# Encoder block on one core: projections as a stage from high and low parts, the delta rule on 64x64 blocks pipelined across units, gate projections in attention

## What is computed

```python
mod = silu(c) @ w_ada + b_ada          # shift1, scale1, gate1, shift2, scale2, gate2
h = rmsnorm(x) * (1 + scale1) + shift1
proj = h @ w_in                        # qkv_a, z_a, beta, alpha, q_b, k_b, v_b, gate_a, gate_b
# A: 4 heads of 128: conv of 5 taps on q, k, v, silu, l2norm of q and k, then per direction,
#    in chunks of 64 tokens (strict, incl: lower triangles; g: cumulated log-decay)
lower = where(strict, beta * (k @ k.T) * exp(g_i - g_j), 0)
u, w = solve(lower + I, [beta * v, beta * exp(g) * k])
for each chunk:                        # S: 128 x 128 state
    v_new = u - w @ S
    o = (q * exp(g)) @ S + (q @ k.T * decay) @ v_new
    S = S * exp(g_last) + (k * exp(g_last - g)).T @ v_new
o_a = rmsnorm(o_forward + o_backward) * gn_w * silu(z)
# B: neighbourhood attention, 8 heads of 64, on the 8 x 64 token grid, window 8 x 16, with a bias
merged = sigmoid(gate_a) * (o_a @ w_oa) + sigmoid(gate_b) * (o_b @ w_ob)
x = x + gate1 * (merged @ w_out)
# then a mixture of 16 SwiGLU experts, each on its top 64 tokens of the group, and a final norm
```

## Time and profile before

| | us |
|---|---|
| median of 3 runs | 2817.16 |
| lowest, highest | 2816.36, 2833.86 |
| the profiled execution | 2837.16 |
| its span, first to last instruction | 2835.4 |

### The profile page before, as it was taken

How to read it: one execution, slowest core, us unless ns; L and a number is a source line. 1 busy time by engine, 2 the same in 40 slices (tenths; PEclk the granted TensorE clock), 3 DMA queues, 4 the chain that set the end, 5 groups by cost and what they waited for, 6 DMA issues and landing times. The chain is left out here.

```text
span 2835.4 us, 32777 instructions
## 1 busy us (share of the span) xinstructions
PE 2648.7 (93%) x11148; PEld 1771.3 (62%) x11148; DVE 1575.7 (56%) x1868; ACT 1177.4 (42%) x1392; POOL 451.4 (16%) x373
## 2 busy tenths in 40 slices
PE   7999999999999997899889859999999999999994
PEld 2465546646564654566334448888888888888883
DVE  2343334434343442344121168888888888888884
ACT  2222121212212221444111137777767776666773
POOL 2022020202110220100122310111111111111101
PEclk9999999999999999555899969999999999999997
DMA  6112301120221111700722169999999999999994
GB/s 209 45 40 65 91 15 60 34 86 19 71 57 49 50 55 40 144 22 0 230 67 111 69 220 357 374 375 373 375 375 374 372 376 377 375 372 378 374 376 163
DMA packets 266085, 539.72 MB, mean 190 GB/s; under 512 B 12297, under 2 KB 65646, under 8 KB 265998
## 3 DMA queue, kind: packets, MB, share of 16 engines
q1 hardware_dynamic: 250125, 498.63, 49.7%
q0 software_dynamic: 4608, 16.78, 2.3%
q10 hardware_dynamic: 11264, 23.14, 2.3%
HBM read 502.82 MB, written 35.68 MB: 190 GB/s over the span
## 5 line engine op out<-in xcount | busy, mean ns | idle before, releaser
L1867 PE MATMUL ps<-whigh,xeT 128*128 128x512 f32 x2048 | 669.1, 400 | 9.2 <-DVE xeT L2012 9.2
L2020 DVE TENSOR_TENSOR wlow<-hT,whigh 128x2048 fp32r<-128x2048 f32 x192 | 432.0, 2284 | 84.7 <-ACT whigh L1963 84.7
L705 PE MATMUL ps<-hT,obT 128*128 128x512 f32 x896 | 442.5, 607 | 17.3 <-ACT obT L884 17.3
L1867 PEld LDWEIGHTS ps<-whigh,xeT 128*128 128x128 f32 x2048 | 387.0, 189 | 100.2 <-issue 9.5
L1867 PE MATMUL ps<-wlow,xeT 128*128 128x512 f32 x1024 | 406.6, 397 | 0.0
L1963 ACT ACTIVATE whigh<-hT 128x2048 fp32r<-128x2048 f32 x192 | 358.5, 1910 | 17.9 <-PE ps L1867 17.9
L1867 PE MATMUL ps<-whigh,hidT 128*128 128x512 f32 x1024 | 334.6, 398 | 1.5 <-DVE hidT L2047 1.5
L2020 DVE TENSOR_TENSOR wlow<-oaT,whigh 128x2048 fp32r<-128x2048 f32 x96 | 216.8, 2286 | 50.2 <-ACT whigh L1963 50.2
L2020 DVE TENSOR_TENSOR wlow<-obT,whigh 128x2048 fp32r<-128x2048 f32 x96 | 217.9, 2284 | 29.6 <-ACT whigh L1963 29.6
L705 PEld LDWEIGHTS ps<-hT,obT 128*128 128x128 f32 x896 | 149.2, 190 | 136.1 <-issue 94.9
L721 PE MATMUL ps<-hT,w 128*128 128x512 f32 x512 | 222.5, 596 | 6.9 <-DVE oaT L1074 3.9
(11 more groups left out here) (271 smaller groups left out, 3283.8 us busy)
## 6 DMA issues: line engine op xcount, KB each, us to landing
hT<-in_w_down SPq DMA_DIRECT2D x66, 1024.0 KB, 8.9
obT<-in_w_up SPq DMA_DIRECT2D x64, 1024.0 KB, 8.8
hT<-in_w_up SPq DMA_DIRECT2D x64, 1024.0 KB, 6.5
hT<-in_w_gate SPq DMA_DIRECT2D x62, 1024.0 KB, 9.3
oaT<-in_w_down SPq DMA_DIRECT2D x62, 1024.0 KB, 6.9
oaT<-in_w_gate SPq DMA_DIRECT2D x34, 1024.0 KB, 9.0
obT<-in_w_gate SPq DMA_DIRECT2D x32, 1024.0 KB, 6.5
ada_d<-in_w_ada SPq DMA_DIRECT2D x8, 2048.0 KB, 9.9
```

Of the source, the lines that this page charges most:

```text
L705: mm = pe.matmul(ps[:, 2, :], we[i % 2][:, k, :], m["hT"][:, k, u * SEQ:(u + 1) * SEQ], start=(k == 0), stop=(k == KD - 1))
L1867: mm = pe.matmul(out, lhs[x], rhs[y], start=start and i == 0, stop=stop and i == 2)
L2020: dve.tensor_tensor(wlow[slot][:, :], raw[(FIRST + x) % RAW_SLOTS], whigh[slot][:, :].bitcast(F32), ALU.subtract).then_inc(low_done, 1)
```

## The change

A stage phase_project is put between prepare and deltanet. It splits hT and each weight tile into high and low fp32r parts and makes all 16 tiles of q, k, v, z and the 12 of attention's q, k, v with three products each. It convolves, applies silu, and stores to conv_dram and early_dram. The norms of q and k are worked out there by squares on GpSimd and matmuls with ones. The later modulation is made by TensorE, with the weights w_ada as the moving operand and four outputs side by side in strips of 32 partitions.

phase_deltanet has no loop and no filler. Each 128x128 block of tokens becomes two 64x64 blocks on partitions 0 to 63 and 64 to 127; small transposes are matmuls with identc. Unit n+1's preparation stands between unit n's levels, scan steps and outputs. The gate projections move to phase_attention, four f32 matmuls behind each slot, kept and stored by ScalarE, with the weights loaded by SyncE. The load of x moves to ScalarE in the merge.

```diff
+                def project(tile, g):
+                    for k in range(KD):
+                        pe.matmul(ps[:, u % 4, :], whi[tile % 3][:, k, :], hh[:, k, cols], start=(k == 0), stop=False)
+                        pe.matmul(ps[:, u % 4, :], whi[tile % 3][:, k, :], hl[:, k, cols], start=False, stop=False)
+                        mm = pe.matmul(ps[:, u % 4, :], wlo[tile % 3][:, k, :], hh[:, k, cols], start=False, stop=(k == KD - 1))
+                def ada_piece(q):
+                    for b in range(4):
+                        mm = pe.matmul(ps[32 * b:32 * b + 32, 5 + half, :], sc32[:, k, :], ada[q % 2][:, b * ADA_BLOCK:(b + 1) * ADA_BLOCK],
+                                       start=(k == 0), stop=(k == KD - 1))
+                def norms(tile):
+                        for t in range(TPG):
+                            mm = pe.matmul(ps[:, 4, col + t:col + t + 1], sq[j % 2][:, t * P:(t + 1) * P], m["ones"][:, 0:1],
+                                           start=True, stop=True)
+                for tile in range(PROJ_TILES):
+                    for g in range(GROUPS):
+                        project(tile, g)
+                    if tile < ADA_PIECES:
+                        ada_piece(tile)
+                    if tile >= 2 and normed(tile - 2):
+                        norms(tile - 2)
...
+                def small_turns(dst, lo, src):
+                    for t in range(TPG):
+                        for half in HALVES:
+                            mm = pe.matmul(ps[half, dst, lo + t * CHUNK:lo + (t + 1) * CHUNK], src[half, t, :], identc[half, :],
+                                           start=True, stop=True)
+                def y(n, lv, d):
+                    for t in range(TPG):
+                        for half in HALVES:
+                            mm = pe.matmul(ps[half, d, t * CHUNK:(t + 1) * CHUNK], xq[n % 2][d][half, 0, t, :], inv[d][half, 0, t, :],
+                                           start=True, stop=True)
+                    mm.then_inc(y_ps[d], 1)
+                    if lv > 0:
+                        small_turns(5 + 2 * d, 0, inv[d][:, 0, :, :]).then_inc(invT_ps[d], 1)
...
+                for n in range(NU):
+                    more = n + 1 < NU
+                    for lv in range(LV):
+                        for d in range(2):
+                            y(n, lv, d)
+                        if lv == 0 and more:
+                            tok_k(n + 1)
+                        if lv == 2 and more:
+                            tok_q(n + 1)
+                        if lv == 2 and n >= 1:
+                            out_turn(n - 1)
+                        for d in range(2):
+                            upd(n, lv, d)
+                        if lv == LV - 1 and more:
+                            rows(n + 1)
+                    uw(n)
+                    scan_kv(n, 0)
+                    if more:
+                        channels(n + 1, 0)
+                        channels(n + 1, 1)
+                    for i in range(1, NCHUNK):
+                        scan_ws(n, i)
+                        if more:
+                            if i == 1:
+                                tok_v(n + 1)
+                            if i == 3:
+                                gram(n + 1, 0)
+                            if i == 4:
+                                qe_turn(n + 1, 0)
+                            if i == 6:
+                                xq_turn(n + 1, 0)
+                        scan_kv(n, i)
+                        if more:
+                            if i == 3:
+                                gram(n + 1, 1)
+                            if i == 4:
+                                qe_turn(n + 1, 1)
+                    for t in range(TPG):
+                        mm = outputs(n, t)
+                        if t == 1 and more:
+                            xq_turn(n + 1, 1)
...
+                    def gates(count):
+                        for _ in range(count):
+                            unit, k = divmod(next(products), KD)
+                            mm = pe.matmul(ps[:, 1, :], wg[i % 2][:, k, :], m["hT"][:, k, u * SEQ:(u + 1) * SEQ],
+                                           start=(k == 0), stop=(k == KD - 1))
                     for w in range(NU + 3):
                         if w < NU:
                             scores(w)
...
+                        if w < NU:
+                            gates(PER_SLOT)
...
+                act.dma_start(m["hT"][:, :, :], a["x"].rearrange("(t p) c -> p t c", p=P)).then_inc(x_in, 16)
                 with act.Fori(0, KD // 2) as jj:
```

More of the change, by code:

```diff
@@ L241, in _ @@
                 sp.dma_start(dtb[:, :], bass.AP(a["dt_bias"].tensor, 0, [[0, P], [1, 2 * HA]])).then_inc(small_in, 16)
-                load_w4(sp, a, first, 0)
+                for tile in range(4):
+                    load_tile(sp, a, first["wraw"], first["w_in"], tile)
             @block.gpsimd
@@ L397, in _ @@
                 for d in range(2):
-                    st.did(dve.tensor_scalar(first["posmask"][:, d, :], m["upto"][:, 1 - d, :], -BIG, BIG, ALU.mult, ALU.add))
+                    for c in range(2):
+                        own = slice(c * CHUNK, (c + 1) * CHUNK)
+                        st.did(dve.tensor_scalar(first["posmask"][own, d, :], m["upto"][own, 1 - d, own], -BIG, BIG,
+                                                 ALU.mult, ALU.add))
                 dve.wait_ge(ssq_done, NT)
@@ L631, in _ @@
[L631 to L633 removed]
+                for n in range(2, NU):
+                    sp.wait_ge(tokv_ps, n - 1)
+                    load_unit(sp, conv_dram, first, n)
+                    sp.wait_ge(oa_done, n - 1)
+                    load_z(sp, conv_dram, first, n)
             @block.gpsimd
             def _(pool):
[L637 to L639 removed]
@@ new lines, in tok_q, with out_turn, rows @@
+                def tok_q(n):
+                    if n >= 2:
+                        pe.wait_ge(on_done, n - 1)
+                    token_major(3, n, 0, tokq_ps)
+                def out_turn(n):
+                    pe.wait_ge(on_done, n + 1)
+                    if n + 2 <= NU:
+                        pe.wait_ge(kn_done, min(n + 3, NU))
+                    turn(2, on, oT_ps)
+                def rows(n):
+                    pe.wait_ge(gsum_done, 2 * n + 2)
+                    pe.wait_ge(kn_done, n + 1)
+                    pe.wait_ge(qn_done, n + 1)
+                    if n >= 2:
+                        pe.wait_ge(oa_done, n - 1)
+                    for d in range(2):
+                        for half in HALVES:
+                            mm = pe.matmul(ps[half, 2 + d, 0:HW], m["ones"][half, 0:CHUNK], gsum[d][half, :, :], start=True, stop=True)
+                        mm.then_inc(row_ps, 1)
```

1299 lines of the change are left out of this document (779 added, 520 removed).

## The result

The changed kernel takes 2697.11 us (median of 4 runs, 2693.53 to 2698.65) against 2816.76 of the kernel before: a ratio of 0.956, 95% interval 0.952 to 0.960. In a later set beside the experiments the same two stood at 2696.69 and 2835.86 us, a ratio of 0.951 (0.949 to 0.952): the kernel before took 2812 to 2817 us in three runs of the first set and 2834 to 2838 in all others, the profiled ones too. The profiled execution took 2698.65 us, its span is 2696.9.

A forecast was written before the change was run, and what follows sets the result against it. TensorE's order was taken to bound the deltanet stage and attention. Deltanet with projections -167, prepare +2, attention +147 and merge +9 summed to -9 us: 2808 us from the 2817.16 median, range 2700 to 2870.

The forecast's parts named there:

- A tiny pass: Delta rule units: each pass of a 64x64 block product costs 0.062 us, with bounds of 0.027 and 0.064.
- the levels' term: Delta rule unit: four levels of 6.0 us and one of 4.0, with token transposes, row sums and mode changes 31 us.
- U: Time of one delta rule unit, eight in the stage: 61 us forecast, bounds 48 and 71.
- 8U - 497: Whole kernel: the change in us as a function of U, all other terms held fixed; -9 us forecast.
- the projection term: New projection stage before the delta rule: 369 us (365 to 410), 314 of them 1344 split products at 0.234.
- The Trainium skill's 62 ns: TensorE: documented floor of about 62 ns per matmul with hardware decode off, taken as agreeing with the trace's 64.
- Rival A: Delta rule units: no floor on tiny passes, halves really pair; U 48 to 52, total 2720 us; chance 0.36.
- attention: Attention with its start, now holding the gate products at 2.4 GHz: 379 us against 232, +147 (130 to 165).
- The scan: Delta rule unit: seven steps of 1.73 us, 12.1, plus 3.2 and 2.6 for next-unit products, less 0.8: 17 us.
- The merge: Merge stage: ScalarE issuing 4 MB of x ahead of its loop adds 9 us (2 to 15).
- Rival B: Delta rule units: without filler they run at 1.2 GHz; U = 71, +71 us, 2888 us; chance 0.14.
- the difference carries over: Whole kernel: -9 us, reckoned on the profiled 2837.16 us, applies equally to the median 2817.16, giving 2808.

## Why the prediction was wrong

- **A tiny pass.** This is the step that failed. The sum took 0.062 us, from the row that is like it "in how long the run is", and kept 0.027 as the other end. The measured price is 0.029: a pass of this form pays for its 64 weight columns, and halves run side by side. What the 2x2 transposes of the earlier trace rows pay their 0.064 for stays open. The paragraph allowed the load of 128 weight columns, but product passes with as many take 0.107 and more at 2.4 GHz; a fixed price of a transposing instruction fits as well. The pairs of the earlier trace rows were the row of the same kind. So the levels' term of 31 us was 17.5. With the low end the paragraph gave U = 48, 2 to 3 us above what was measured; 1.6 of that is its scan.
- **The size.** With U = 46.1 the forecast's 8U - 497 is -128 and the profiled time 2709; the 10 us to the measured 2699 are the projection term (-11).
- **The Trainium skill's 62 ns** stood beside the sum and doesn't hold for a pass, as shown above; it agreed with the row that the sum wrongly went by.
- **Rival A** (no floor, 2720 us, 0.36) is what happened; its U of 48 to 52 was still 2 us or more too long.
- **The outputs** (6.5, measured 6.3), **the preparation of unit 0** (15, measured 14.0), **attention** (379, measured 383.7) and the **slot** (5.0, measured 5.09) were right, each from the prices in the earlier trace rows. So was the jump of the clock in attention. The scan (17, measured 15.4) was 1.6 us too long: its bare step of 1.73 came out (1.74 at 2.4 GHz), the 5.8 us added for the next unit's products were too many. The projection stage was put 11 us too long, 9 of them in its products.
- **The merge** was right in size (+9, measured +10.4 by TensorE's own stretch) and wrong in place: "a longer first wait". The first wait grew by 1.2 us, the second round's by 8.5.
- **Rival B** was held off by something the forecast had in its sum and not in its argument: with the next unit's products in the scan the clock stays up, without them it falls, as the pipelining undone shows.
- **What sets the old stage.** The forecast read "TensorE is busy 1007 of 1038.5 us" as a stage set by TensorE's order. With 336 us of passes gone it was 67 shorter. The sum didn't rest on that reading, since it was built up from the new unit's own steps.
- **The median.** The sum was made on the profiled 2837 us and 20 us were taken off on the claim that "the difference carries over". It doesn't: the changed kernel has 2697 as median and 2699 profiled. The kernel before was profiled once more to find the stage that makes the 20 us; it took 2838.2 us, with attention and merge starting within 1 us of where they started before, so the stage stays open. The change is worth 120 us by the first set and 139 by the second.

## What to carry to other kernels

Price small f32 matmuls by their weight columns: in these rows a product pass takes what the larger of weight columns and moving columns takes (0.107 to 0.111 us for 128, 0.429 for 512, at 2.4 GHz), two halves of the array run beside each other when they are issued in turn, and a row of the same form and halves outweighs a row that only resembles it in length. Before moving filler, ask what it costs where it stands: take it out once. Here the levels, bound by their chain, held it for nearly nothing (6.08 us against 6.16) and the scan didn't (1.73 us a step against 2.90). A stretch of light steps should have something wide or dense in it, for the clock as much as for the time.

## What the runs showed of the hardware

- At 1.2 GHz a product pass with 128 weight columns takes 0.214 us with 8 and with 64 moving columns, and 0.212 with weights of 2 rows.
- Alternating halves with 64 weight columns take 0.029 us a pass at 2.4 GHz with 8 moving columns as with 64.
- TensorE busy without a gap isn't enough for the clock: it fell to 0.50 in a run of passes with 8 columns, busy 5.47 of 5.47 us, and stayed there through 13.70 us of full weights with 64 columns.
- A scan step takes 1.74 us at 2.4 GHz and 2.31 at 1.2. So a scan with nothing in it took 14.8 us, one with the next unit's products 14.9, and the one bare scan that kept most of its clock 12.3.
- Passes for different halves start beside each other even when they aren't neighbours: 3.79 us for a level whose halves stand in blocks of 8 passes, against 3.14 alternating.
- 32 needless passes a level cost the stage 17 us or 23 instead of 30, by which execution of the changed kernel they are held against.
- The 2x2 transposes, with 128 weight columns, start every 0.064 us at 2.4 GHz, where a product with as many takes 0.107 (half of 0.214). Whether the transposing form loads faster or pays a fixed price wasn't tested.
